# Output projection of a layer in three parts: where each part of the sum is taken

## The reference, cut to what matters

```python
x = x + 0.5 * swiglu(rmsnorm(x, ffn1_norm), ...)
h = rmsnorm(x, mix_norm) @ w_in
o_a = chunk_relpos_attention(...)   # 6 heads: 384 channels, rows 0:384 of w_out
o_b = dsa_attention(...)            # 5 heads, each query sees its 256 best keys
o_c = mla_attention(...)            # 5 heads
x = x + jnp.concatenate([o_a, o_b, o_c], axis=-1) @ w_out     # 1024 x 1024
x = x + 0.5 * swiglu(rmsnorm(x, ffn2_norm), ...)
```

## Time and profile before

| | us |
|---|---|
| median of 3 runs (range) | 4116.31 (4113.97 to 4118.38) |
| the profiled execution, its own time | 4122.55 |
| span of the profile | 4120.8 |
| second attention, layer 0 (692 to 820) and layer 1 (1896 to 2026) | 128 and 130 |
| rest of the output projection, layer 0 (820.7 to 848.2) | 27.5 |

### The profile page before, as it was taken

How to read it: one execution, slowest core, us unless ns; L and a number is a source line. 1 busy time by engine, 2 the same in 40 slices (tenths; PEclk the granted TensorE clock), 3 DMA queues, 4 the chain that set the end, 5 groups by cost and what they waited for, 6 DMA issues and landing times.

```text
span 4120.8 us, 48423 instructions
## 1 busy us (share of the span) xinstructions
PE 3855.2 (94%) x17196; PEld 3050.2 (74%) x17196; DVE 1940.8 (47%) x3222; ACT 1490.6 (36%) x2451; POOL 381.7 (9%) x332
## 2 busy tenths in 40 slices
PE   8999997799999999987899998899999999899999
PEld 6887664588888887665688886777777768677877
DVE  4433467654334423567554344335544444645652
ACT  3222343432223223333432234436535553533221
POOL 0100001101001101011011021101000000100110
PEclk9999998899999999987899999999999989999999
DMA  4333221033333333211133333131122113223332
GB/s 119 96 97 108 69 59 47 10 100 97 97 91 92 97 97 109 59 44 34 40 94 95 106 114 91 40 87 44 47 72 62 47 43 93 74 82 87 97 92 97
DMA packets 484448, 321.89 MB, mean 78 GB/s; under 512 B 10928, under 2 KB 464176, under 8 KB 483280
## 3 DMA queue, kind: packets, MB, share of 16 engines
q1 hardware_dynamic: 479616, 301.81, 25.2%
q0 software_dynamic: 3536, 16.13, 1.2%
q10 hardware_dynamic: 1152, 2.10, 0.1%
HBM read 310.82 MB, written 8.52 MB: 77 GB/s over the span
## 4 chain that ended last, share of the span: by engine, by line
PE 73%; DVE 8%; ACT 7%; issue 6%; DVEq 4%; POOLq 0%; DMA 0%; ACTq 0%; POOL 0%; SPq 0%
PE bank L234 21%; PE bank L236 20%; PE bank L235 20%; ACT w_hi L219 2%; DVE w_lo L226 1%; PE bank L1188 1%; PE bank L2152 1%; DVEq L2455 1%; PE bank L1199 1%; PE bank L1191 1%; PE bank L1190 1%; PE bank L1172 1%; PE bank L974 1%; DVEq L2469 1%; DVEq L1013 1%
## 5 line engine op out<-in xcount | busy, mean ns | idle before, releaser
L234 PE MATMUL bank<-h_hi,w_hi 128*128 128x512 f32 x3064 | 1230.0, 401 | 68.3 <-DVE h_lo L386 24.9
L226 DVE TENSOR_TENSOR w_lo<-w_raw,w_hi 128x1024 fp32r<-128x1024 f32 (+1 forms) x571 | 742.4, 1301 | 1070.8 <-ACT w_hi L219 1067.5
L236 PE MATMUL bank<-h_lo,w_hi 128*128 128x512 f32 x3128 | 1230.1, 393 | 0.0
L235 PE MATMUL bank<-h_hi,w_lo 128*128 128x512 f32 x3064 | 1204.7, 393 | 0.0
L219 ACT ACTIVATE w_hi<-w_raw 128x1024 fp32r<-128x1024 f32 (+1 forms) x571 | 591.5, 1038 | 620.0 <-DMA w_raw<-in_ffn_w_down 316.6
L234 PEld LDWEIGHTS bank<-h_hi,w_hi 128*128 128x128 f32 x3064 | 579.6, 189 | 236.8 <-issue 101.4
L236 PEld LDWEIGHTS bank<-h_lo,w_hi 128*128 128x128 f32 x3128 | 591.4, 189 | 131.3 <-issue 2.3
L235 PEld LDWEIGHTS bank<-h_hi,w_lo 128*128 128x128 f32 x3064 | 579.3, 189 | 114.5 <-issue 2.0
L234 PE MATMUL bank<-g_hi,w_hi 128*128 (+1 forms) x880 | 343.7, 391 | 3.7 <-DVE gu_ring L2471 3.7
L235 PE MATMUL bank<-g_hi,w_lo 128*128 (+1 forms) x880 | 343.4, 390 | 0.0
L236 PE MATMUL bank<-g_lo,w_hi 128*128 (+1 forms) x880 | 343.3, 390 | 0.0
(11 more groups left out here) (438 smaller groups left out, 4628.7 us busy)
## 6 DMA issues: line engine op xcount, KB each, us to landing
w_raw<-in_w_in SPq DMA_DIRECT2D x105, 512.0 KB, 3.8
w_raw<-in_ffn_w_gate SPq DMA_DIRECT2D x88, 512.0 KB, 3.8
w_raw<-in_ffn_w_up SPq DMA_DIRECT2D x88, 512.0 KB, 3.8
w_raw<-in_ffn_w_down SPq DMA_DIRECT2D x88, 512.0 KB, 3.5
w_raw<-in_w_mix SPq DMA_DIRECT2D x50, 512.0 KB, 3.9
w_raw<-in_w_up SPq DMA_DIRECT2D x44, 512.0 KB, 3.8
w_raw<-in_w_branch SPq DMA_DIRECT2D x32, 512.0 KB, 3.7
w_raw<-in_w_down SPq DMA_DIRECT2D x22, 512.0 KB, 3.2
```

The source lines that it names most:

```text
L226: dve.tensor_tensor(WL[:, slot(c), 0:w], RAW[:, slot(c), 0:w], WH[:, slot(c), 0:w].bitcast(F32), ALU.subtract).then_inc(w_lo, 1)
L234: pe.matmul(bank, wh, xh, start=start, stop=False)
L235: pe.matmul(bank, wl, xh, start=False, stop=False)
L236: return pe.matmul(bank, wh, xl, start=False, stop=stop)
```

## The change

The output projection is cut in three. The A part keeps its eight pieces and its matmuls, and they move to steps 2, 4, 6, ..., 16; DVE adds each in the hook of the step after. Tiles 6 and 7 (heads C1 to C4) become a second part: eight pieces of six matmuls in steps 21, 23, ..., 35, added to x by DVE in steps 22, 24, ..., 36. A `drain` follows each of the 16 additions. The rest, tiles 3, 4 and 5, is nine matmuls for each m behind the attention. The weights: three units of 1024 columns for A as before, two of 1024 for tiles 6 and 7 (split in steps 10 and 18), and six for the rest, of 384, 384, 768, 768, 384 and 384 columns (the first two split in steps 30 and 33); 11 units as before. Every unit of the ring keeps its place, so the last load but three of the projection still frees the slot of the first feed-forward unit.

```diff
-U_WO = U_WOA + 3
-U_FFN2 = U_WO + KT
+U_WOB = U_WOA + 3
+U_WO = U_WOB + 2
+OUT_TILES = ((0,), (1,), (2, 3), (4, 5), (6,), (7,))
+U_FFN2 = U_WO + len(OUT_TILES)
...
-        for m in range(KT):
-            load(sp, q, U_WO + m, raw_tile(U_WO + m, 5, P),
-                 w_out[3 * P:8 * P, m * P:(m + 1) * P].rearrange("(k p) c -> p k c", p=P))
+        for k in range(2):
+            load(sp, q, U_WOB + k, RAW[:, slot(U_WOB + k), :], w_out[(6 + k) * P:(7 + k) * P, :])
+        for u, ms in enumerate(OUT_TILES):
+            w = len(ms) * P
+            load(sp, q, U_WO + u, raw_tile(U_WO + u, 3, w),
+                 w_out[3 * P:6 * P, ms[0] * P:ms[0] * P + w].rearrange("(k p) c -> p k c", p=P))
...
+    OUT_PARTS = sorted([(2 + 2 * m, "a", m) for m in range(KT)] + [(21 + 2 * m, "cb", m) for m in range(KT)])
+
+    def parts_at(n):
+        return [(j, which, m) for j, (at, which, m) in enumerate(OUT_PARTS) if at == n]
+
+    def part_output_pe(pe, l, q, j, which, m):
+        tiles, unit = ((0, 1, 2), U_WOA) if which == "a" else ((6, 7), U_WOB)
         if m == 0:
-            split_ready(pe, q, U_WOA + 2)
-            pe.wait_ge(y_lo, l * 8 + (3 + 2))
-        pe.wait_ge(wa_done, l * KT + (m + 1))
-        for k in range(3):
+            split_ready(pe, q, unit + len(tiles) - 1)
+            pe.wait_ge(y_lo, l * 8 + (3 + 2 if which == "a" else 3 + 2 + 2))
+        pe.wait_ge(wa_done, l * 2 * KT + (j + 1))
+        for a, k in enumerate(tiles):
...
         if m == KT - 1:
             pe.drain()
-            pe.sem_inc(w_used, 3)
+            pe.sem_inc(w_used, len(tiles))
...
-        dve.tensor_tensor(x_tile(m), B[(5, 7)[m % 2]][:, :], x_tile(m), ALU.add).then_inc(wa_done, 1)
+        dve.tensor_tensor(x_tile(m), B[(5, 7)[j % 2]][:, :], x_tile(m), ALU.add).then_inc(wa_done, 1)
+        dve.drain()
...
+    def layer_out_dve(dve, q):
+        dve.drain()
+        for u, ms in enumerate(OUT_TILES):
+            lo(dve, q, U_WO + u + AHEAD)
+            dve.wait_ge(w_used, q * RING + (U_WO + u + 5))
+            for m in ms:
+                dve.tensor_tensor(x_tile(m), B[m % 4][:, :], x_tile(m), ALU.add).then_inc(x_done, 1)
...
-    OUT_SPLITS = {16: 0, 38: 1}
+    OUT_SPLITS = {10: U_WOB, 18: U_WOB + 1, 30: U_WO, 33: U_WO + 1}
...
-            if n % TT == 3 and n // TT < KT:
-                a_output_dve(e, l, n // TT)
+            for j, which, m in parts_at(n - 1):
+                part_output_dve(e, l, j, m)
...
-            if n % TT == 2 and n // TT < KT:
-                a_output_pe(e, l, q, n // TT)
+            for j, which, m in parts_at(n):
+                part_output_pe(e, l, q, j, which, m)
```

More of the change, by code:

```diff
@@ L206, in load @@
         sp.dma_start(dst, src).then_inc(raw_in[slot(c)], 16)
-    UNIT_WIDTH = {U_UQ: 864, U_UQ + 1: 576, U_UKV: 640, U_UKV + 1: 640, **{U_WO + m: 640 for m in range(KT)}}
+    UNIT_WIDTH = {U_UQ: 864, U_UQ + 1: 576, U_UKV: 640, U_UKV + 1: 640, **{U_WO + u: 384 * len(ms) for u, ms in enumerate(OUT_TILES)}}
     def load_cols(sp, q, c, w, c0):
@@ L1391, in bias_dve @@
         dve.drain()
-    def a_output_pe(pe, l, q, m):
+    OUT_PARTS = sorted([(2 + 2 * m, "a", m) for m in range(KT)] + [(21 + 2 * m, "cb", m) for m in range(KT)])
[3 more added lines that the diff above has]
+        tiles, unit = ((0, 1, 2), U_WOA) if which == "a" else ((6, 7), U_WOB)
         if m == 0:
-            split_ready(pe, q, U_WOA + 2)
-            pe.wait_ge(y_lo, l * 8 + (3 + 2))
-        pe.wait_ge(wa_done, l * KT + (m + 1))
-        for k in range(3):
+            split_ready(pe, q, unit + len(tiles) - 1)
+            pe.wait_ge(y_lo, l * 8 + (3 + 2 if which == "a" else 3 + 2 + 2))
+        pe.wait_ge(wa_done, l * 2 * KT + (j + 1))
+        for a, k in enumerate(tiles):
             yh, yl = y_tile(k)
-            last = products(pe, B[(5, 7)[m % 2]][:, :], U_WOA + k, slice(m * P, (m + 1) * P), yh, yl, k == 0, k == 2)
+            last = products(pe, B[(5, 7)[j % 2]][:, :], unit + a, slice(m * P, (m + 1) * P), yh, yl, a == 0,
+                            a == len(tiles) - 1)
         last.then_inc(wa_mm, 1)
@@ L1405, in a_output_pe, with part_output_dve, layer_out_pe @@
             pe.drain()
-            pe.sem_inc(w_used, 3)
-    def a_output_dve(dve, l, m):
-        dve.wait_ge(wa_mm, l * KT + (m + 1))
-        if m == 0:
+            pe.sem_inc(w_used, len(tiles))
+    def part_output_dve(dve, l, j, m):
+        dve.wait_ge(wa_mm, l * 2 * KT + (j + 1))
+        if j == 0:
             dve.wait_ge(x_back, l * 16 + 16)
-        dve.tensor_tensor(x_tile(m), B[(5, 7)[m % 2]][:, :], x_tile(m), ALU.add).then_inc(wa_done, 1)
+        dve.tensor_tensor(x_tile(m), B[(5, 7)[j % 2]][:, :], x_tile(m), ALU.add).then_inc(wa_done, 1)
+        dve.drain()
+    def layer_out_pe(pe, l, q):
+        pe.wait_ge(y_lo, l * 8 + (8 + 2))
+        for u, ms in enumerate(OUT_TILES):
+            split_ready(pe, q, U_WO + u)
+            for a, m in enumerate(ms):
+                if m >= 4:
+                    pe.wait_ge(x_done, l * XL + 2 * KT + (m - 3))
+                for k in range(3):
+                    yh, yl = y_tile(3 + k)
+                    c0 = (k * len(ms) + a) * P
+                    last = products(pe, B[m % 4][:, :], U_WO + u, slice(c0, c0 + P), yh, yl, k == 0, k == 2)
+            last.then_inc(w_used, 1)
+    def layer_out_dve(dve, q):
+        dve.drain()
+        for u, ms in enumerate(OUT_TILES):
+            lo(dve, q, U_WO + u + AHEAD)
+            dve.wait_ge(w_used, q * RING + (U_WO + u + 5))
+            for m in ms:
+                dve.tensor_tensor(x_tile(m), B[m % 4][:, :], x_tile(m), ALU.add).then_inc(x_done, 1)
     def out_sp(sp, q, c, w):
@@ L1539, in out_hook @@
             if n in OUT_SPLITS:
-                hi(e, q, U_WO + OUT_SPLITS[n])
+                hi(e, q, OUT_SPLITS[n])
         attend_act(act, cb_steps, l * N_STEPS + N_A, l * HEADS + 6, l * JOBS + len(a_jobs), layer_y, cb_jobs,
                    lambda j: [(post_done, l * N_POSTS + (N_POSTS + 2)), (k4_in, l * 16 + 16)], IN_CB, hook=out_hook)
-        for m in range(KT):
-            hi(act, q, U_WO + m + AHEAD)
+        for u in range(len(OUT_TILES)):
+            hi(act, q, U_WO + u + AHEAD)
         gained_act(act, l * 2 + 1, lambda k: vl_at(l, V_FFN2 + k),
@@ L1586, in out_hook @@
             if n in OUT_SPLITS:
[L1587 removed]
+                lo(e, q, OUT_SPLITS[n])
             next_round(rounds, 1 if n < B_FROM - 1 else N_ROUNDS if n == B_FROM - 1 else 0)
[L1589 to L1590 removed]
+            for j, which, m in parts_at(n - 1):
+                part_output_dve(e, l, j, m)
         attend_dve(dve, cb_steps, l * N_STEPS + N_A, l * 8 + 3, layer_y, IN_CB, hook=out_hook)
[L1592 removed]
+        layer_out_dve(dve, q)
         gained_dve(dve, l * 2 + 1, lambda k: vl_at(l, V_FFN2 + k))
@@ L1682, in out_hook @@
         def out_hook(e, n):
-            if n % TT == 2 and n // TT < KT:
-                a_output_pe(e, l, q, n // TT)
+            for j, which, m in parts_at(n):
+                part_output_pe(e, l, q, j, which, m)
         attend_pe(pe, cb_steps, l * N_STEPS + N_A, l * N_STEPS + N_A, l * HEADS + 6, l * JOBS + len(a_jobs), l * 8 + 3,
                   IN_CB, hook=out_hook, banks=1)
-        out_pe(pe, q, U_WO, l * XL + 2 * KT, lambda e, k: e.wait_ge(y_lo, l * 8 + (8 + 2)),
-               [y_tile(k) for k in range(3, 8)])
+        layer_out_pe(pe, l, q)
         ffn_pe(pe, q, U_FFN2, l * 2 + 1)
```

## The result

The changed kernel takes 4145.58 us (median of 4, 4140.18 to 4152.45) against 4115.14 (4113.73 to 4118.38) for the one before in the same session: ratio 1.0078 [1.0064, 1.0093], 30 us slower. The forecast of 4128 had the side right and 40% of the size; the time lies above its range.

The account below looks back on a forecast made before the run. It took PE to bound the end, and a closed DVE-ACT-PE loop the attention. Per layer 14.65 us won, 19.75 lost: 10.2 slower for both layers, 4126.5, plus 1.5 to 2 of clock: 4128 us, range 4110 to 4141.

Parts of the forecast that it names:

- The shorter end: Behind each attention: 48 of 120 matmuls leave, 11.0 us won per layer.
- the stall: Behind the attention: second feed-forward unit loads late, delaying the last addition; 2.1 us lost per layer, bounds 0 to 2.7.
- step 38: Late in the attention: a weight split removed there lets the mask follow the lo part sooner; 1.95 us won per layer.
- The additions: DVE inside the attention: sixteen instead of eight, twelve paid at 0.75; 9.3 us lost per layer with drains.
- The split of step 30: Inside the attention: added split of 384 columns, 0.5 on ACT and 0.55 on DVE, priced at 0.55 us.
- The piece of step 21: PE inside the attention: new six-matmul piece, not covered because that step also waits for the pair's lo part; 0.5 us lost.
- the pieces removed from n%4 = 2: Steps 18 to 30: scores no longer wait behind A pieces; 0.7 us won in layer 0, 2.7 in layer 1.
- One or two sets more at the low level: Head sets inside both attentions: longer PE waits lower the clock, 1.4 us each, 1.5 to 2 us lost.
- Rival (a): More PE work inside the attention keeps full clock: seven sets gain 1.4 us each, giving 4114; chance 0.18.
- rival (c): More is paid: low clock in sets of steps 23 to 35 and behind the stall, late load; 4140; 0.20 with (d).
- (b): Additions and splits fall in DVE's idle time inside the attention: 27 us come back, giving 4101; chance 0.12.
- (d): The end behind the attention stays bound by loads, so its 11.0 us is not won; 0.20 with rival (c).

Follow-up runs that it names:

- again: The changed kernel once more, unmodified, for a second profile; 4147.21 us, ratio 1.0069 to the kernel before.
- before_filler: The kernel before, plus matmuls whose result nothing reads, ahead of all ten head sets of a layer; 4099.51 us, ratio 0.9970.
- after_filled: The changed kernel, plus matmuls whose result nothing reads, 5 to 12 ahead of each head set; 4130.79 us, ratio 1.0022.
- a_part_alone: The kernel before with only the A part moved to steps 2, 4, ..., 16, no drains; 4140.15 us, ratio 1.0051.
- no_drain: The changed kernel without the drain behind its sixteen additions; 4141.63 us, ratio 1.0057.

## Why the prediction was wrong

Against the median of before the loss is 30 us, by again 28; the steps gave 12, 10.2 of terms and 1.8 of clock. Both parts were too small.

*What held.* The shorter end (11.0, measured 10.9), the stall (2.1; PE's wait grew by 2.3 and 2.1), step 38 (1.95, 1.96), the splits of steps 10 and 18 (1.75 each; measured 1.6 and 1.5) and that of step 33 where PE has the full clock (0.6; 0.55). In layer 0, at the low level, the distance from mask 32 to mask 33, which holds it, grew by 2.1.

*The first step that failed: the terms inside the attention.* They are read from the two kernels with unread products, from the mask of step 0 to that of step 39, first before_filler, then after_filled:

```profile
696.78 0.29 DVE L1258 CUSTOM_DVE_ANT_0 s_ring<-bank,mask 128x128 f32<-128x128 f32 x1 [0.61 <-issue]
803.53 0.68 DVE L1258 CUSTOM_DVE_ANT_0 t_ring<-bank,b_select 128x512 f32<-128x512 f32 x1
```

```profile
699.48 0.29 DVE L1263 CUSTOM_DVE_ANT_0 s_ring<-bank,mask 128x128 f32<-128x128 f32 x1 [0.61 <-issue]
826.30 0.68 DVE L1263 CUSTOM_DVE_ANT_0 t_ring<-bank,b_select 128x512 f32<-128x512 f32 x1
```

106.75 and 126.82 us, and the same in layer 1: 20.1 more in each. The terms give 9.3 + 4.65 + 3.7 - 1.95 - 1.7 = 14.0, so 6.1 are missing in each layer. Three terms were too small. The additions: nine of the twelve paid ones show 0.95, two 0.78 and one, in round 26, only 0.2; with 0.35 for each of the four that were counted as free this is 11.7, not 9.3. The split of step 30: 1.15 more than its 0.55, because it was priced by its columns alone; ahead of it stand ACT's operands, and beside it POOL. The piece of step 21: 1.1 at the full clock instead of 0.5. Together 4.1. And the 1.7 for the pieces removed from n%4 = 2 is not won beside that. Round 26's addition is cheap because the piece that left step 26 gives 0.77 back (the distance of that step fell from 2.70 to 1.93 in a_part_alone). Of the 2.7 read in layer 1, 2.0 lay in one step, from mask 21 to mask 22, 4.00 long in before and 2.00 in before_filler with its pieces in place. That makes 5.8 of the 6.1. With the shorter end and the stall as measured the terms come to 23 us by the traces, not 10.2; by the times the two repaired kernels differ by 1.0022 less 0.9970, 21 us, and with the two intervals by 14 to 29.

*The second: the clock.* "One or two sets more at the low level" was 1.8 us. The sets took 4.0 more. The reading that misled was that the wait directly ahead of a set decides its level, 2.60 us against 1.40, and that pieces taken from steps 18 to 30 are only work saved. In a_part_alone, where nothing else changed, steps 20 to 36 of layer 0 became 3.4 us longer, where the forecast had the removed pieces as 0.7 won. PE waits only 0.40 ahead of step 23's set there, and the set is low. Here is that first matmul, the set, and the 10 us before it:

```profile
774.49 0.77 PE L1188 MATMUL bank<-cb_turned_hi,pair_v_hi 128*128 128x512 f32 x1 [0.40 <-DVE cb_turned_lo L1270]
```

```profile
764.50:774.50 10.00, 9.60 (x33) 6.83 (x31) 5.18 (x18) 5.31 (x15) 2.49 (x3) 0.50 0.00 0
774.40:777.80 3.40, 3.31 (x11) 3.06 (x12) 1.70 (x4) 0.81 (x2) 1.55 (x2) 0.50 0.02 5
```

PE busy for 9.60 of 10 us and still low, with 33 matmuls; before had 43 in the 10 us ahead of that set, at 1.00:

```profile
755.40:765.40 10.00, 8.40 (x43) 6.24 (x44) 7.05 (x24) 6.16 (x17) 2.48 (x3) 1.00 0.01 2
```

At the low level PE's busy time is long because each matmul is longer (in before those of 512 columns start 0.43 apart at 0.50, from 695.14 to 698.56, so nine take 3.9 us, where the prediction's half clock had twice 2.06; behind the attention, at 1.00, they start 0.23 apart), so in these rows neither busy time nor the last wait tells the level. Unread products raised it in both kernels: the twenty sets took 46.5 us instead of 65.1 (after_filled) and 42.2 instead of 61.1 (before_filler). Rival (a) had more matmuls in the attention and so a higher clock. But the new pieces are six matmuls where nine had stood, and the mean came to 0.77 and 0.80, from 0.82 and 0.79. Why the pieces of six held the level less well was not tested by itself.

How large the change's own part is: repairing the clock gives 0.0047 of the ratio in the changed kernel (1.0069 to 1.0022), 19 us, and 0.0030 in the one before, 12 us. The difference is 7 us, but with the intervals of the three runs it lies anywhere from -5 to 19. The traces agree with the middle: from mask 0 to mask 39 the unread products take 9.9 and 9.5 us off the changed kernel and 4.7 and 8.0 off the one before, 6.8 us apart. The products behind the new stall, 2.8 us here and 4.2 in again, come on top. The sum had nothing for them, though rival (c) priced them at 2 x 1.7. Against this, the rest of the projection in layer 1 began at the low level before (0.50 from 2026.00 to 2029.50; its 120 matmuls took 30.3 us instead of 27.5) and no longer does. So the clock's part is some 7 to 8 us by the traces, where 1.8 was forecast: less than what the terms missed.

*The rivals.* (a) had the lever right and its direction wrong. (b) fell: the additions and splits were paid. (c) came nearest with 4140, and in part by its own means: the sets of steps 23 to 35 took 4.6 us more where it had 7, the products behind the stall 2.8 to 4.2 where it had 3.4, and the late load did not come. (d) did not happen.

## What to carry to other kernels

In a loop closed over three engines, read the clock level before and after as a term of its own: matmuls that look like ballast in front of a critical set may be what keeps the level up. Moving eight A pieces to steps 2 to 16 took the twenty sets from 61.1 to 71.2 us and the kernel 21 us up (a_part_alone). Give products behind a new stall a price at the low level, here 2.8 us for the first fifteen. Price an inserted instruction by the whole distance to the next useful start (drain, the producer's queue, what runs on POOL beside it), not by its columns: here 0.95 us for an addition put at 0.75, and 1.7 for a split put at 0.55. Before restructuring, try the cheap repair first: unread products in PE's waits gave 0.3% here on the unchanged kernel, and the restructured one with the same products and three more mends came no lower.

## What the runs showed of the hardware

An explicit drain between an addition and the next operation of DVE moved that start from 0.61 to 0.95 us, and without it (no_drain) it was 0.60. Two of DVE's operations were longer beside one of POOL's: the lo part of 384 columns above (0.81 instead of 0.55), and a scaling of 256 columns took 1.32 us in round 22 (788.51, beside POOL's 1.26 from 788.41), where before it took 0.35:

```profile
788.51 1.32 DVE L1270 TENSOR_SCALAR s_ring<-s_ring,row_sum_reciprocal 128x256 f32<-128x256 f32 x1
```

TensorE stayed at the low level behind a stretch in which PE was busy for 9.60 of 10 us at 0.50 (a_part_alone), and fell to it behind a wait of 3.80 us that followed 16 us of matmuls at 1.00 (the changed kernel, layer 0; first product 0.77 us, 0.50 from 873.40 to 877.00), though not behind one of 3.67 in layer 1 (first product 0.47).
